# Expert weight loads on one core: two w_down transfers of 128 partitions split into 112, 8 and 8

## What is computed

```python
def expert_block(args):
    xb, e = args
    hgu = xb @ w_gu[e] + b_gu[e]
    gate = jnp.minimum(hgu[:, :D_EXPERT], SWIGLU_LIMIT)
    up = jnp.clip(hgu[:, D_EXPERT:], -SWIGLU_LIMIT, SWIGLU_LIMIT)
    act = (up + 1.0) * gate * jax.nn.sigmoid(SWIGLU_ALPHA * gate)
    return act @ w_down[e] + b_down[e]
```

## Time and profile before

| | |
|---|---|
| median of three runs | 1136.52 us (1135.8 to 1137.64) |
| span of the profiled execution | 1136.2 us |
| TensorE matmul busy | 1093.1 us, 96% |
| VectorE, ScalarE busy | 263.5 us, 139.7 us |
| read from HBM | 433.84 MB, 383 GB/s over the span |
| SP's DMA queue (q1) | 434.15 MB, 91.1% of 16 engines' span |

### The profile page before, as it was taken

One profiled execution on the slowest core, in us unless ns is written; L12 is line 12 of the kernel. 1 busy time (PEld: TensorE's weight loads), 2 busy tenths in 40 slices (PEclk: granted clock), 3 DMA queues, 4 the chain that ended last, 5 costly groups with the idle time before them and its releaser, 6 DMA issues.

```text
span 1136.2 us, 11432 instructions
## 1 busy us (share of the span) xinstructions
PE 1093.1 (96%) x5084; PEld 477.8 (42%) x5084; DVE 263.5 (23%) x618; ACT 139.7 (12%) x240; POOL 9.6 (1%) x20
## 2 busy tenths in 40 slices
PE   8999999999999999999999979999999998999998
PEld 5677778543333333333333324333333333333332
DVE  3665422232111111111111111221111111111111
ACT  1415342010000000000000000000000000000001
POOL 1100000000000000000000000000000000000000
PEclk9999999999999999999999997999999998999999
DMA  9466537789999999999999999999999999999996
GB/s 275 155 240 212 204 134 321 295 351 422 434 428 432 437 434 437 428 430 434 427 434 435 430 418 427 429 431 433 430 433 430 432 434 430 433 422 430 425 424 248
DMA packets 34018, 435.64 MB, mean 383 GB/s; under 512 B 5328, under 2 KB 6512, under 8 KB 20176
## 3 DMA queue, kind: packets, MB, share of 16 engines
q1 hardware_dynamic: 33456, 434.15, 91.1%
q0 software_dynamic: 96, 0.08, 0.2%
q10 hardware_dynamic: 416, 0.66, 0.2%
HBM read 433.84 MB, written 1.05 MB: 383 GB/s over the span
## 4 chain that ended last, share of the span: by engine, by line
PE 75%; DMA 21%; DVE 2%; ACT 1%; issue 0%; SPq 0%; ACTq 0%; DVEq 0%
PE Pp L908 34%; DMA gate_up_room<-in_w_gate_up 19%; PE Bp L922 12%; PE Pp L609 7%; PE Ap L936 4%; PE Pp L597 3%; PE Bp L894 3%; PE Pp L790 2%; PE Ap L801 2%; PE Pp L643 1%; PE Bp L915 1%; DMA odd_down<-in_b_down 1%; DVE odd_down L1437 1%; PE Pp L850 1%; PE Bp L882 1%; PE Pp L922 1%
## 5 line engine op out<-in xcount | busy, mean ns | idle before, releaser
L908 PE MATMUL Pp<-gate_up_room,OBT 128*64 128x512 f32 x2048 | 455.2, 603 | 17.3 <-DMA gate_up_room<-in_w_gate_up 17.3
L908 PEld LDWEIGHTS Pp<-gate_up_room,OBT 128*64 128x64 f32 x2048 | 146.9, 139 | 309.6 <-issue 283.5
L1426 DVE TENSOR_SCALAR odd_down<-Pp 128x512 f32<-128x512 f32 x31 | 21.4, 692 | 624.0 <-PE Pp L908 624.0
L922 PE MATMUL Bp<-even_down,odd_down 128*64 128x512 f32 x512 | 113.6, 595 | 1.2
L922 PE MATMUL Bp<-odd_down 128*64 128x512 f32 x480 | 106.3, 595 | 1.8 <-DVE odd_down L1437 0.6
L609 PE MATMUL Pp<-odd_down,gate_up_room 128*128 128x256 f32 x384 | 85.2, 380 | 0.0
L1636 ACT ACTIVATE odd_down<-odd_down 128x512 f32<-128x512 f32 x30 | 18.9, 630 | 477.1 <-DVE odd_down L1426 477.1
L609 PEld LDWEIGHTS Pp<-odd_down,gate_up_room 128*128 128x128 f32 x384 | 72.1, 190 | 10.9 <-issue 1.1
L936 PE MATMUL Ap<-odd_down,cst 64*128 64x512 f32 x256 | 64.6, 623 | 4.9 <-DMA odd_down<-in_b_down 4.2
L922 PEld LDWEIGHTS Bp<-even_down,odd_down 128*64 128x64 f32 x512 | 35.3, 137 | 68.8 <-issue 64.1
L922 PEld LDWEIGHTS Bp<-odd_down 128*64 128x64 f32 x480 | 33.1, 137 | 65.3 <-issue 60.0
(11 more groups left out here) (215 smaller groups left out, 627.7 us busy)
## 6 DMA issues: line engine op xcount, KB each, us to landing
gate_up_room<-in_w_gate_up SPq DMA_DIRECT2D x27, 2048.0 KB, 39.3
even_down<-in_w_down SPq DMA_DIRECT2D x11, 4096.0 KB, 36.9
odd_down<-in_w_down SPq DMA_DIRECT2D x11, 4096.0 KB, 39.4
gate_up_room<-in_w_gate_up SPq DMA_DIRECT2D x10, 4096.0 KB, 22.3
gate_up_room<-in_w_in SPq DMA_DIRECT2D x8, 2048.0 KB, 7.9
even_down<-in_w_down SPq DMA_DIRECT2D x7, 2048.0 KB, 16.9
odd_down<-in_w_down SPq DMA_DIRECT2D x6, 2048.0 KB, 20.7
odd_down<-in_w_down SPq DMA_DIRECT2D x7, 1024.0 KB, 20.9
```

Source lines behind the costliest of these rows:

```text
L908: last = mm((Gps, Ups)[q // 2][64 * (q % 2):64 * (q % 2) + 64, :], xT[:, k % 4, k // 4, :], quarter(e, w, q), start=False, stop=k == KC - ...
L922: last = mm(bank[64 * hf:64 * hf + 64, :], turned[:, c, s, :], w[:, c * 1024 + hf * 512:][:, 0:512], start=s == 0 and c == 0, stop=s == DN ...
L1426: V.tensor_scalar(gm, Gps, LIMIT, None, ALU.min).then_inc(d_gm, 1)
```

## The change

Two constants are added, `TILTED = (10, 18)` and `MORE = 112`. For experts 10 and 18 the one transfer of w_down becomes three, in this order: partitions 0 to 111, partitions 112 to 119, partitions 120 to 127. Each adds 16 to the same semaphore, and the count that TensorE waits for rises by the same (`1 + (128 - 112) // 8` = 3 transfers).

```diff
+TILTED = (10, 18)
+MORE = 112
...
             if i < GU and e in JOINED:
                 return 1 if i == 0 else 0
+            if i == GU and e in TILTED:
+                return 1 + (P - MORE) // 8
             if e in (WHOLE if i < GU else EIGHT):
                 return 1 - i % 2
...
                 if e in EIGHT:
                     released(e, TURNS - 1)
-                    sp.dma_start(downs[e % 2], dn_rows(e)).then_inc(full(e, GU), 16)
+                    rows_of = [slice(0, P)]
+                    if e in TILTED:
+                        rows_of = [slice(0, MORE)] + [slice(p, p + 8) for p in range(MORE, P, 8)]
+                    for r in rows_of:
+                        sp.dma_start(downs[e % 2][r, :], dn_rows(e)[r, :]).then_inc(full(e, GU), 16)
                     return
```

## The result

The changed kernel takes 1176.07 us (median; 1170.41 to 1183.75) against 1136.17 us of the kernel before on the same chip: a ratio of 1.0348, 95% interval 1.0325 to 1.0371. It is slower by 3.5%, in the direction forecast, 24 us above the 1152 us of the forecast and 4 us past the upper end of the range. The profiled execution took 1170.41 us, the fastest of the four, with a span of 1168.6 us against 1136.2: 32.4 us more to find in the trace, where the medians differ by 39.9.

A forecast was written before the change was run, and what follows sets the result against it. TensorE and DMA loads were taken to bound the kernel in turn, with no idle DMA time in load-bound stretches. Two changed loads at +9.0 us, less 2 us lead: 1136.2 + 18.0 - 2 = 1152.2 us, range 1134.5 to 1172 us.

The forecast's parts named there:

- the three signs: Expected in the changed profile: expert 11's gate/up wait 7 to 9 us longer, such waits near 33 us, under 433 GB/s near full share.
- the 8 rows: Each 8-partition w_down transfer of experts 10 and 18 was priced at 5.1 us, between ends of 1.2 and 6.4 us.
- the bias loads: Three 32-partition loads early in the earlier trace, 205 GB/s against 407 at like engine share, used to price narrow transfers.
- the 112 rows: The wide w_down part for experts 10 and 18 was taken at full rate, 8.5 us; the other end was 17.0 us.
- The wide part is not what it says: Rival: 112 rows spread unevenly or meeting at partitions, up to 8.5 us more per changed load, about 1169.5 us; chance 0.13.
- late next are gate/up of 11 to 15: Claim that lateness shows first in gate/up loads of experts 11 to 15, then of 19 to 25; no separate size.
- issue and wait: Four more SP-queue issues, 1.3 us, and TensorE's wait for three transfers were taken as hidden, at nothing.
- What is covered: Lead of engines carrying the small loads absorbs 0 to 3 us of the 18 us loss; 2 us taken.
- s: Time of one small 8-row load on its engine, 4 to 6.4 us in the forecast's own range.
- Balance: Rival: small loads cost a usual row on engines mostly ahead, sparing the slowest 2.4 us: 1134.1 us; chance 0.14.
- Hidden: Rival: with a small load near 1.5 us, gain and loss cancel, 1136.5 us within 2.3; chance 0.10.
- Half speed only: Rival: each small load takes 2.4 us, adding 7.2 us less 0 to 3, near 1142 us; chance 0.11.

## Why the prediction was right and wrong

**Right: the direction, and the bound.** The loads had no idle engine time to give, lost transfer time passed in full to the end, twice, and nothing behind the last load-bound wait changed. Two of the three signs named for it were seen: 223 and 151 GB/s at a share of 1 or above after load 10, and a wait at expert 11 that is 9.0 us longer (7 to 9 were named). That agreement is partly luck, since gate/up of 10 and w_down of 10 had already pushed TensorE back by 5.2 us (525.03 against 519.79). The third, the sum of these waits, rose further than was named, to 42.6 us and not to near 33.

**Right: the 8 rows.** The forecast took 5.1 us for each; the pair measured alone gives 5.2. The price that was drawn from the bias loads in the earlier trace rows, by the partitions reached, carried over to a transfer a quarter as wide. That the reason is the same is not shown: by the partitions reached, 64 would get 205 x 64 / 32 = 410 GB/s, and they got 210.

**Wrong: the 112 rows.** The step that failed is "I take 8.5, since all full-width rows run at one rate". It treated 112 partitions as nearly full width and put the half rate aside as the other end of the bound. Measured alone, the part stands for 19.6 us, at 213 to 220 GB/s. With its own other end, 17.0, the sum would have been 17.0 + 10.2 - 9.7 = 17.5 us a load, 35 less 2 in all, 1169.2 us: beside the 1168.6 of the profiled span (the median lies 7 us higher). The rival that said this, *The wide part is not what it says*, gave 1169.5 us and had a chance of 0.13. "Nothing in the trace shows such a split" held as much against the price that was taken: no row of before showed any transfer of 112 partitions, and the nearest narrow one was halved.

**Short: its size even so.** 19.6 us is above 17.0, which was the end of that bound. Part of it is in a place that the forecast did not look at: it said "late next are gate/up of 11 to 15", what is queued behind. Gate/up of 10, queued ahead, is the first to be waited for, 3.71 us in the changed kernel, 6.99 us with the small transfers alone and 3.05 us with the 112 rows alone. The 2.9 us that the 112 rows lose beyond the half rate, with 2.2 MB of wide transfers moving beside them, are about the 2.6 us that lie above the bound; how they divide between what is ahead and what is behind was not separated.

**Right: issue and wait.** They were costed at nothing. Three transfers cut by columns give 1.0005.

**What is covered** was taken as 2 us of lead on some engines. No run shows a lead that pays for anything. A mean share of 0.56 does not say that seven engines are done and nine at work, and the assumption under it, one row to one engine with a ninth on eight of them, is not visible in any view. Even shares (112 and 16) cost nearly as much.

**The range of the forecast itself** does not follow from its ends: s from 4 to 6.4 us and a lead of 3 to 0 us make 1136.2 + 13.6 - 3 = 1146.8 to 1136.5 + 23.2 = 1159.7 us, not 1144 to 1163. The measured time is above both.

**The rivals.** *Balance* falls, as do *Hidden* and *Half speed only*: more rows for some engines, by partitions or by columns, adjacent or spread, were slower each time. Why it could not work is argued from the runs, not shown: if the loads fill the destination evenly, each group of partitions gets the same bytes in every split, and giving more of them to an engine that is ahead moves no byte to another destination.

**An explanation** that fits all the runs, and is not shown to be the only one, is that a transfer moves at the full 433 GB/s when it writes equally many partitions in every group of four adjacent ones (128, every second, every fourth), and at about half where it doesn't (every eighth, every seventh of 112, 64 or 96 adjacent), even if only a few groups are left out (112, 120). Three sets of rows stand on the fast side. For sets that reach half of the groups this is what a full destination looks like.

The Trainium skill has that case (SBUF — State Buffer, Door 1: The DMA port swizzle): 64 adjacent partitions reach eight of 16 ports, no more than 32 do, with an asymptote of 218 GB/s; the halves agree, with 210. For partitions 0 to 111 the same map has a part of every port, and counting ports alone would not halve them: 213 to 220 GB/s measured, so there the page does not say enough.

It may be the order in which the engines take the rows. The Trainium skill (DMA: Bandwidth & Descriptors, The descriptor swizzle) says that in a transfer of 128 partitions each engine writes to one port of its own. The page does not list the rows of other shapes, and no view here names an engine. If 112 adjacent rows are dealt out otherwise, engines may meet at a port; this is argued, not shown. That the step of seven is as slow as the adjacent 112 doesn't decide it. This stays open.

No version beats both kernels. The pieces that are free gain nothing, as the DMA carries 433 GB/s already.

## What to carry to other kernels

Where the DMA runs at its limit, split a load by columns, so that each piece still writes all 128 partitions, or by every second or fourth partition; a block of adjacent partitions, be it 112 of 128, went at about half the rate and slowed the wide transfers around it. Look for that in GB/s beside the DMA share: full share at half the bytes means that the engines are held up, not idle, and here evening out their shares (112 and 16) did not help. Where a shape is absent from the trace and the nearest row is bad, take the price from that row, and measure the shape alone in one run.

## What was not expected of the hardware

- 112 of 128 adjacent partitions are no better than 64, nor are 120 with 8 behind them: 220, 210 and 174 GB/s from 500 to 510 us, where the loads before carry 433.
- Four transfers of 32 partitions, four apart, cost nothing (1.0007), eight of 16, eight apart, cost 2.9%.
- Two transfers of 0.26 MB cost as much as one of 4.19 MB (1.0012): 105 and 144 GB/s in all for 10 us, with the transfer ahead of them late too.
- The times of the changed kernel scatter over 13 us (1170.41 to 1183.75), those of the kernel before over 2 us. Why was not looked into.
